# A 16-expert mixture summed on chip in open PSUM banks, with the activated rows turned inside the next up projection

## What is computed

```python
def grouped_moe(x, router_w, router_bias, w_gate, w_up, w_down):
    ...                       # best group of 4 experts, then the top 2 in it: gate[token, expert]
    y = jnp.zeros_like(t)
    for e in range(N_EXPERTS):
        h = jax.nn.silu(t @ w_gate[e]) * (t @ w_up[e])
        y = y + gate[:, e:e + 1] * (h @ w_down[e])
    return y.reshape(b, s, d)
...
        ffn = grouped_moe(x, ...)
        x = layernorm(DN_ALPHA * x + ffn, p['ln2_g'][l], p['ln2_b'][l])
```

## Time and profile before

| | us |
|---|---|
| three runs: lowest, median, highest | 917.15, 918.55, 918.9 |
| profiled execution, first to last instruction | 916.5 |
| layer 0, first up projection starts to last down projection's end | 224.29 to 449.07 |
| layer 1, the same | 674.66 to 896.18 |
| PE busy | 793.1 |
| DVE busy | 335.0 |
| ACT busy | 187.3 |

### The profile page before, as it was taken

One profiled execution on the slowest core, in us unless ns is written; L12 is line 12 of the kernel. 1 busy time (PEld: TensorE's weight loads), 2 busy tenths in 40 slices (PEclk: granted clock), 3 DMA queues, 4 the chain that ended last, 5 costly groups with the idle time before them and its releaser, 6 DMA issues.

```text
span 916.5 us, 9955 instructions
## 1 busy us (share of the span) xinstructions
PE 793.1 (87%) x3943; PEld 387.2 (42%) x3943; DVE 335.0 (37%) x749; ACT 187.3 (20%) x452; POOL 44.0 (5%) x58
## 2 busy tenths in 40 slices
PE   6978999998899886876879989979898999777875
PEld 4665777453433222222334567654534333222221
DVE  1016455445422212122281054654533442122138
ACT  1213343110321101110110025620103211111101
...
DMA  9724007736999999999799060581679999999991
GB/s 357 232 72 196 1 1 297 300 153 239 402 424 423 425 428 422 425 426 424 265 350 361 3 261 1 215 330 53 275 282 424 431 423 429 422 428 423 428 398 57
DMA packets 43552, 272.80 MB, mean 298 GB/s; under 512 B 6360, under 2 KB 11166, under 8 KB 25840
## 3 DMA queue, kind: packets, MB, share of 16 engines
...
...
## 4 chain that ended last, share of the span: by engine, by line
PE 56%; DMA 25%; DVE 9%; SPq 6%; ACT 2%; issue 1%; ACTq 0%; DVEq 0%
DMA arena<-in_expert_w_up 24%; PE bank L916 16%; PE bank L858 6%; PE bank L930 5%; PE bank L1176 5%; PE bank L845 3%; SPq L502 2%; PE bank L832 2%; PE bank L777 2%; PE bank L939 2%; PE bank L1049 2%; PE bank L825 1%; PE bank L679 1%; PE bank L1141 1%; PE bank L868 1%
## 5 line engine op out<-in xcount | busy, mean ns | idle before, releaser
L916 PE MATMUL bank<-arena 128*64 128x512 f32 x1024 | 240.7, 627 | 48.2 <-DMA arena<-in_expert_w_up 46.5
L916 PEld LDWEIGHTS bank<-arena 128*64 128x64 f32 x1024 | 77.2, 144 | 208.4 <-issue 148.8
L930 PE MATMUL bank<-arena 128*64 128x512 f32 x512 | 116.9, 598 | 16.7 <-DVE arena L1825 16.7
L1825 DVE COPY arena<-bank 128x256 f32<-128x256 f32 x32 | 13.6, 424 | 271.8 <-PE bank L923 271.8
L930 PEld LDWEIGHTS bank<-arena 128*64 128x64 f32 x512 | 34.1, 136 | 77.4 <-issue 54.6
L1378 ACT ACTIVATE arena<-bank 128x256 f32<-128x256 f32 x32 | 12.3, 384 | 265.8 <-PE bank L916 265.8
L1833 DVE RECIPROCAL arena<-arena 128x256 f32<-128x256 f32 x32 | 56.1, 1753 | 1.1
L858 PE MATMUL bank<-arena 128*128 128x512 f32 x128 | 56.0, 595 | 0.0
L1176 PE MATMUL bank<-arena 128*128 128x512 f32 x96 | 43.9, 619 | 6.6 <-ACT arena L1483 5.7
L1234 ACT COPY arena<-bank 128x512 f32<-128x512 f32 (+2 forms) x30 | 15.8, 537 | 112.9 <-PE bank L679 74.2
L858 PEld LDWEIGHTS bank<-arena 128*128 128x128 f32 x128 | 24.0, 190 | 29.6 <-issue 29.5
...
## 6 DMA issues: line engine op xcount, KB each, us to landing
...
expert_rows<-arena ACTq DMA_DIRECT2D x60, 128.0 KB, 7.9
...
```

The lines of the kernel that those rows point to most:

```text
L916: last = mm(bank[j][64 * half:64 * half + 64, :].rearrange("p (u f) -> p u f", u=2), slots[:, k, 0:CAP], w[:, :, k, 256 * half:256 * half ...
L930: last = mm(bank[3 + j][64 * n:64 * n + 64, :], hid_t[:, j, c, 64 * half:64 * half + 64], w[:, half, c, 512 * n:512 * n + 512], start=(hal ...
```

## The change

What it does:

- The outputs of all 16 experts stay on chip. ACT copies each into one half of `y_pair` (`keep`), and PE adds each pair of experts into five PSUM banks that stay open over the layer (`add_pair`): a 128 x 288 matrix `hot` holds each token's gate in the row of its slot. DVE forms it (`hots`) from rows that PE spreads at the start (`spread_rows`). The scaled x is added by PE as well (`add_x`). The stores, `bring_back` and DVE's additions go.
- The sum of pair p stands in front of up 2p+3 (for p of 2 and more), behind up 2p+3 (for p of 0 and 1), and the last one behind down 15.
- The turn of expert e-1 moves from behind up e into its middle, after 8 of its 16 products, for e from 3 on.
- The weights of the last expert's up projection come in two halves with a semaphore each, and those of the down projections too; up 15 begins with the first half.
- Down projections now share bank 2 (the last has bank 0), and the next one waits for `keep` of the one before. memx1 and memkv1 use banks 1 and 2 in place of 5 to 7, and memx1's four copies are all ACT's, behind the square root of the first tile. The sample tile's sum goes from PSUM to SBUF by four ACT copies before that square root.

```diff
         def sum_bank(t, c):
-            return bank[((0, 1), (5, 6), (2, 7))[t][c]]
+            return bank[((5, 6), (3, 4), (7, 7))[t][c]]
+
+        def down_bank(e):
+
+            return bank[0 if e == NE - 1 else 2]
...
             yield "up", 2
             for e in range(3, NE):
+                if e % 2 and e >= 7:
+                    yield "sum", (e - 3) // 2
                 yield "up", e
+                if e % 2 and e < 7:
+                    yield "sum", (e - 3) // 2
                 yield "down", e - 1
             yield "down", NE - 1
...
+            def load_last_up(l, halves):
+
+                for h, s in enumerate(halves):
+                    ks = slice(4 * h, 4 * h + 4)
+                    for u, name in enumerate(("expert_w_gate", "expert_w_up")):
+                        src = ins[name][l, NE - 1].rearrange("(p k) f -> p k f", k=KC)
+                        sp.dma_start(ups[(NE - 1) % 3][:, u, ks], src[:, ks, :]).then_inc(s, 16)
...
                         sp.wait_ge(up_done, NE * l + e + 1)
-                        load_up(l, e + 3, ups[e % 3], up_in[e % 3])
+                        if e + 3 < NE - 1:
+                            load_up(l, e + 3, ups[e % 3], up_in[e % 3])
+                        else:
+                            load_last_up(l, last_up_in)
...
             experts(0, "kq2", "kq2", "outb0")
-            sp.wait_ge(down_done, NE)
-            sp.wait_ge(back_in[0], 32)
+            sp.wait_ge(down_done, NE - 2)
             load_kvs(0)
...
+            def spread_rows(l):
+
+                pe.wait_ge(starts_ready, l + 1)
+                for i in (TURNS - 2, TURNS - 1):
+                    pe.wait_ge(*turn_taken(l, i))
+                for t, (a, n) in enumerate(TOKS):
+                    for q, v in enumerate((row_ab, gates)):
+                        for s in range(2):
+                            c = n * (2 * q + s)
+                            last = tr(bank[5 + t][:, c:c + n], v[0:n, s, t:t + 1].broadcast_to([n, P]), ident[0:n, 0:n])
+                    last.then_inc(spread_turned, 1)
+
+            def add_x(l, t):
+
+                a, n = TOKS[t]
+                pe.wait_ge(x_scaled, l + 1)
+                if t < 2:
+                    for c in range(2):
+                        mm(sum_bank(t, c)[:, :], ident, x_tok[:, t, 512 * c:512 * c + 512], start=False, stop=False)
+                else:
+                    for c in range(4):
+                        mm(sum_bank(2, 0)[DEC * c:DEC * (c + 1), 0:D // 4], ident[0:n, 0:n],
+                           x_tok[0:n, 2, D // 4 * c:D // 4 * (c + 1)], start=False, stop=False, tile_position=(0, DEC * c))
+
+            def add_pair(l, p):
+
+                pe.wait_ge(hot_ready, NP * l + p + 1)
+                pe.wait_ge(kept, 2 * (NE * l + 2 * p + 2))
+                for t in (0, 2, 1):
+                    a, n = TOKS[t]
+                    v = hot[:, p % 2, a:a + n]
+                    if t < 2:
+                        for c in range(2):
+                            last = mm(sum_bank(t, c)[:, :], v, y_pair[:, c, :], start=p == 0, stop=p == NP - 1)
+                    else:
+                        for c in range(4):
+                            last = mm(sum_bank(2, 0)[DEC * c:DEC * (c + 1), 0:D // 4], v,
+                                      y_pair[:, c // 2, D // 4 * (c % 2):D // 4 * (c % 2 + 1)],
+                                      start=p == 0, stop=p == NP - 1, tile_position=(0, DEC * c))
+                    if p == NP - 1:
+                        last.then_inc(tile_ready, 1)
+                if p < NP - 1:
+                    last.then_inc(summed, 1)
+
             def experts(l):
+                def turn_hidden(e):
+
+                    pe.wait_ge(h_ready, NE * l + e + 1)
+                    expert_turn(e % 2).then_inc(ht_ready, 1)
+
                 def up(e):
-                    pe.wait_ge(up_in[e % 3], 32 * loads(l, e))
+                    if e < NE - 1:
+                        pe.wait_ge(up_in[e % 3], 32 * loads(l, e))
...
-                    expert_up(e % 2, ups[e % 3], xg[:, e % 2]).then_inc(up_done, 1)
+                    for half in range(2):
+                        if e == NE - 1:
+                            pe.wait_ge(last_up_in[half], 32 * (l + 1))
+                        last = expert_up(e % 2, ups[e % 3], xg[:, e % 2], range(4 * half, 4 * half + 4))
+                        if half == 0 and e > 2:
+                            turn_hidden(e - 1)
+                    last.then_inc(up_done, 1)
                 def down(e):
                     at = NE * l + e + 1
-                    pe.wait_ge(h_ready, at)
-                    expert_turn(e % 2).then_inc(ht_ready, 1)
+                    if not 1 < e < NE - 1:
+                        turn_hidden(e)
                     pe.wait_ge(ht_copied, at)
-                    pe.wait_ge(dn_in[e % 3], 32 * loads(l, e))
-                    if e > 1:
-                        pe.wait_ge(y_copied, copied(l, e - 2))
-                    elif l and PAIR[l - 1]:
-                        pe.wait_ge(pair_copied, 4 * pairs(l))
-                    elif l:
-                        pe.wait_ge(y_copied, copied(l - 1, NE - 2 + e))
-                    expert_down(e % 2, dn[e % 3]).then_inc(down_done, 1)
+                    if 0 < NE * l + e and e < NE - 1:
+                        pe.wait_ge(kept, 2 * (NE * l + e))
+                    for half in range(2):
+                        pe.wait_ge(dn_in[e % 3][half], 16 * down_loads(l, e))
+                        last = expert_down(down_bank(e), e % 2, dn[e % 3], [half])
+                    last.then_inc(down_done, 1)
...
-                def store(e):
-
-                    j, at = e % 2, NE * l + e + 1
-                    if stores(l, e) > 1:
-                        ac.wait_ge(y_stored[j], 32 * (stores(l, e) - 1))
-                    ac.wait_ge(down_done, at)
-                    nc.scalar.copy(y_out[:, j, :], bank[3 + j][:, :]).then_inc(y_copied, 1)
-                    ac.wait_ge(y_copied, copied(l, e))
-                    for n in range(2):
-                        ac.dma_start(y_dram[CAP * e:CAP * (e + 1), 512 * n:512 * n + 512],
-                                     y_out[64 * n:64 * n + 64, j, :]).then_inc(y_stored[j], 16)
-
                 def keep(e):
-                    j, at = e % 2, NE * l + e + 1
-                    ac.wait_ge(down_done, at)
+                    j = e % 2
+                    ac.wait_ge(down_done, NE * l + e + 1)
                     for n in range(2):
                         nc.scalar.copy(y_pair[64 * j:64 * j + 64, n, :],
-                                       bank[3 + j][64 * n:64 * n + 64, :]).then_inc(pair_copied, 1)
+                                       down_bank(e)[64 * n:64 * n + 64, :]).then_inc(kept, 1)
...
-                if l == 0:
-                    copies("memx1", mem_dst(mem_feat1))
+                ac.wait_ge(tile_ready, 3 * l + 2)
+                for c in range(4):
+                    own(nc.scalar.copy(x_tok[0:DEC, 2, D // 4 * c:D // 4 * (c + 1)],
+                                       sum_bank(2, 0)[DEC * c:DEC * (c + 1), 0:D // 4]), sample_moved if c == 3 else None)
                 memkv1 = jobs("memkv1")
                 for t in range(3):
                     if l == 0 and t == 1:
                         copies("x2a", feat_dst)
                     root(2 * l + 1, t)
+                    if l == 0 and t == 0:
+                        copies("memx1", mem_dst(mem_feat1))
                     if l == 0 and t < 2:
                         k, b = next(memkv1)
...
+                def hots(p):
+
+                    if NP * l + p >= 2:
+                        ve.wait_ge(summed, max((NP - 1) * l + p - 1, (NP - 1) * l))
+                    if l and p < 2:
+                        ve.wait_ge(tile_ready, 3 * l)
+                    h, at = hot[:, p % 2, :], cst("slot")[:, p:p + 1]
+                    own(stt(h, spread[:, 0, :], at, spread[:, 2, :], ALU.is_equal, ALU.mult))
+                    step(stt(hot_b, spread[:, 1, :], at, spread[:, 3, :], ALU.is_equal, ALU.mult))
+                    own(tt(h, h, hot_b, ALU.add), hot_ready)
...
                 form(2)
+                for t, (a, n) in enumerate(TOKS):
+                    ve.wait_ge(spread_turned, 3 * l + t + 1)
+                    own(V.tensor_copy(spread[:, :, a:a + n], bank[5 + t][:, 0:4 * n].rearrange("p (q n) -> p q n", n=n)))
+                own.settle()
+                hots(0)
                 for e in range(3, NE):
                     turned(e - 1)
                     form(e)
...
-                    if e == NE - 2:
+                    if e % 2:
+                        hots(e // 2)
+                    if e == 4:
                         ve.wait_ge(x_sorted, 96 * (l + 1))
                         for t in range(3):
-                            own(ts(x_tok[:, t, :], x_tok[:, t, :], ALPHA, None, ALU.mult))
```

(19 more changed lines are left out.)

195 lines of the change are left out of this document (71 added, 124 removed).

## The result

The changed kernel takes 935.27 us in the median of four runs (929.23, 935.04, 935.5 and 937.56) against 918.59 us: a ratio of 1.0181, 95% interval 1.0138 to 1.0225, so it is slower by 1.4 to 2.3%. A ratio leaves out runs of a known slower kind that a median holds, so it isn't always the quotient of the medians. I had forecast 925.0 us and a range from 911 to 934. The profiled execution is the fastest of the four, with a span of 927.4 us against 916.5 before and the forecast's 922.9.

The account below looks back on a forecast made before the run. PE, not the weight stream, was to bound the mixtures: 37.7 us of PE work replaces 34.2 of slack in layer 0. Layers +0.7 and +5.7 make +6.4: 922.9 profiled, 925.0 with 2.05 around it; range 911 to 934.

Parts of the forecast that it names:

- layer 0's tail: End of down 15 to end of kvs0: 46.0 us against 48.8 before, a gain of 2.8.
- Turn inside up: Turn in the middle of an up takes 0.43 us; gain 0.6 for experts 2 to 13, 7.2 a layer.
- Five waits of 1.5 us: Sums 2 to 6, right behind a down, wait for ACT's copies: 1.5 us five times, 7.5 a layer.
- Sums: Sums of pairs 0 to 6 on PE: 3.95 us each, 27.6, plus 0.3 each for shape changes, 2.1 a layer.
- spread_rows: PE's wait for the last two row copies, about 0.7 us, and 12 transposes at 0.12: 2.2 us a layer.
- a copy of equal length: In the mixtures ACT's `keep` replaces a copy of equal length; no size given.
- rival 3: Clock: regular 1.5 us waits lower the granted clock, ten ups pay 1.7 us each, 942 us; chance 0.06.
- Down 15: Last down of a layer: wait behind its turn taken as 0.52 us; in layer 0 it ends 3.5 us later.
- DVE's new work lies under PE: In the mixtures DVE's three 288-wide passes a pair are covered by PE's work; no size given.
- Up 3's turn: Waits 1.1 us for DVE, as up 3 follows up 2 with no down between.
- turn 15: Must wait until 4.6 us after up 15 ends, so moving turn 14 gives nothing back and costs 0.4.
- memkv1's start: In layer 0's tail memkv1 starts 9.4 us behind down 15, before 5.3.

Follow-up runs that it names:

- no_sums: Changed kernel without six of the seven sums inside each mixture and without the scaled x; outputs wrong, whole time 2775 us, mixtures 192.6 and 193.3 us.
- turn_behind_up: Changed kernel with each turn again directly ahead of its down, behind the up projection: 945.46 us, ratio 1.0309 to the kernel before.
- sum_behind_up: Changed kernel with the sums of pairs 2 to 6 behind up 2p+3 instead of ahead of it: 916.04 us, ratio 0.9947 to the kernel before.
- warm_spread: Changed kernel plus one unread 512-column product on PE ahead of the spreading transposes: 930.21 us, ratio 1.0121 to the kernel before.
- hots_late: Changed kernel with DVE forming a layer's last one-hots behind the last turned copy instead of ahead of it: 932.41 us, one run.
- tail_order: Changed kernel with both of ACT's memkv1 copies together, ahead of the second tile's square root in layer 0: 928.43 us, ratio 1.009 to the kernel before.
- again: The changed kernel once more, unedited, in a second series: 936.59 us, ratio 1.019 to the kernel before.

## Why the prediction was wrong

The direction held, and so did the mechanism of the mixtures: PE's own chain bounds both, the weights are in time and lie under it by some 19 us a layer (no_sums; I had said 14), and the 10 to 14 us a layer that the stream can give are bought with more than that on PE. The time came out 10 us above the forecast and outside its range. Two things failed: the step on layer 0's tail, together with small terms of the sum that were wrong or missing, 4.5 us in the profiled execution; and the step from one execution's time ahead of the mixture to every other's, the other 6. By the steps of the sum:

- **Turn inside up**: 0.43 us in the rows, as I took it; but up costs 0.05 more for being cut, 0.6 us a layer (turn_behind_up).
- **Five waits of 1.5 us**: right, 1.49 each. sum_behind_up takes them away and the core is 7.9 us a layer shorter. This is what makes the change a loss: without these waits it is faster than the kernel before.
- **Sums**: 4.40 us, not 4.25: 0.15 x 7, 1 us a layer too little. I had counted 0.3 for the three groups of a sum, and they cost 0.45.
- **spread_rows**: the spreading costs 2.2 us, as forecast (3.23 us from the last turning of sorted rows to the turn, 1.02 before). Yet from down 0 to down 1 it takes only 1.5 us more, 12.62 against 11.08, since that turning waits 0.43 us for ACT where it waited 1.03. I had called ACT's `keep` a copy of equal length; it takes 1.18 us against 0.59, but the two issues of stores behind the old copy, 1.19 us, are gone. And I left out the clock behind it: +1.7 us in layer 0 and +2.8 in layer 1. My rival 3 asked whether the regular 1.5 us waits lower the clock, and they don't (1.00 from 302 to 430 us); a shorter one, 0.80 us among several, does at this place, and warm_spread shows it.
- **Down 15**: I took the wait behind its turn as 0.52 and it was 1.18, as DVE's last one-hots stand ahead of the copy: +0.66 us a layer (hots_late). I had written that DVE's new work lies under PE. At the last expert nothing of PE covers it.
- **Up 3's turn and turn 15** cost less than I said, by 1.1 and 0.9 us. Up 3's turn comes 3.6 us behind the end of up 2 and turn 15 3.7 behind that of up 15. The 4.6 that I took for this path is only the turn and down of expert 14, which stood in between the earlier trace rows: turn 15 followed down 14 at once, so that row showed PE's own work and no wait for DVE.
- **Layer 0's tail**, the largest single step that failed: "the 5.72 us of waiting ahead of it [...] are gone, since memkv1's bank is no longer the one that kvs0 needs". The wait remained, 3.09 us. ACT's copies out of the banks share one counter, and PE waits for kvs0's input by a number on it. memkv1's second copy has its place in that number whichever bank it empties, and ACT makes it last. The start of kvs0 came 31.5 us behind that of down 15 (29.4 before). tail_order, which changes only the place of that copy, shows it: 0.83. Another 0.6 us is memkv1's start, 10.0 us behind down 15 and not 9.4. That kvs0 then keeps its pace (20.9 us) was luck: of the nine profiled executions with this wait of 3.1 us it took 20.87 in the two of the changed kernel and 22.56 in the other seven, as in sum_behind_up (the row below), while behind 0.83 us it took 20.84 in all four.

```profile
473.91 22.56 PE L1226 MATMUL bank<-arena 128*128 128x512 f32 x48 [3.09 <-ACT arena L1521]
```

In layer 0's mixture these come to 0.6 + 1.05 - 0.7 + 1.7 + 0.66 - 1.1 - 0.9 = 1.3 us (missing in the table: 1.5), in layer 1's to 2.4 (2.7). With the tail's 2.7 and 0.2 at the end, less the 2.4 us by which this execution reached up 0 sooner, that is, but for roundings, the 4.5 us between the two sums of the table. Those 2.4 us are luck of the same kind as what follows.

The other 6 us lie between the profiled run and the median: the profiled execution was the fastest of its kernel, and in `again`, the only other one of this kernel with a profile, the first mixture starts 5.7 us later. The forecast carried one execution's way to up 0 over to the changed kernel; one trace couldn't show how much that stretch varies. What sets it stays open: the instructions ahead of the first down 0 are the same in all kernels here, but for 4 KB of constants, and yet its start lies at 239.19 us before, at 236.79 and 242.53 in two profiled executions of the changed kernel, and from 233.55 to 245.18 in the others. From 0 to 220 us the granted clock is 0.94 in the first and 0.91 in the second. The two stretches, first execution above (PE to POOL busy, clock, DMA share, GB/s):

```profile
0.00:220.00 220.00, 200.21 (x1130) 131.72 (x1131) 85.82 (x250) 56.09 (x161) 18.16 (x26) 0.94 0.49 185
...
0.00:220.00 220.00, 200.09 (x1118) 132.84 (x1119) 84.42 (x249) 55.72 (x160) 14.33 (x22) 0.91 0.48 180
```

PE is busy for as long, and gets less far. Most of the 5.7 us arises in one place: around 82 us the second execution is 1.2 us behind, and 5.6 at the products of L840, which start at 94.11 and 99.73 us. In between the granted clock is 1.00 in the first (81.0 to 94.1 us) and 0.71 in the second (82.0 to 99.7 us). The same products in both:

```profile
90.30 3.89 PE L833 MATMUL bank<-arena 128*64 128x272 f32 x32
...
93.62 6.18 PE L833 MATMUL bank<-arena 128*64 128x272 f32 x32
```

Of the 14 profiled executions the eight with a clock of 0.94 to 0.96 in this stretch reach down 0 between 233.6 and 239.2 us, the six with 0.91 to 0.93 between 240.3 and 245.2. Why the median of one kernel lies nearer to its fast end than that of another (tail_order's ten runs all lie under again's six, by more than the rows explain) stays open too. The cores of the mixtures don't vary, and they carry the readings above.
